# Two layers with a chunked two-way scan: the state part of a chunk placed beside the inverse of the next chunk

## The reference

```python
def rwkv_scan(state0, f, d, reverse):
    ...
    def step(S, inp):
        r_t, w_t, k_t, v_t, kk_t, b_t = inp
        sa = -jnp.einsum("bhvk,bhk->bhv", S, kk_t)
        S = S * w_t[:, :, None, :] + sa[..., None] * b_t[:, :, None, :] + v_t[..., None] * k_t[:, :, None, :]
        return S, jnp.einsum("bhvk,bhk->bhv", S, r_t)
```

## Time and profile before

| what | value |
|---|---|
| median of three runs | 2203.51 us |
| the runs | 2200.98 to 2205.61 us |
| span of the profiled execution (first to last instruction) | 2192.6 us |
| share of the span in which PE was busy | 89% |
| share of VectorE, ScalarE, GpSimd | 47%, 34%, 14% |
| mean granted TensorE clock | 0.954 |
| scan of layer 0, first to last matmul | 213.1 to 436.9 us |
| scan of layer 1, first to last matmul | 1462.7 to 1678.5 us |

### The profile page before, as it was taken

How to read it: one execution, slowest core, us unless ns; L and a number is a source line. 1 busy time by engine, 2 the same in 40 slices (tenths; PEclk the granted TensorE clock), 3 DMA queues, 4 the chain that set the end, 5 groups by cost and what they waited for, 6 DMA issues and landing times. The chain is left out here.

```text
span 2192.6 us, 51555 instructions
## 1 busy us (share of the span) xinstructions
PE 1952.2 (89%) x22829; PEld 1569.6 (72%) x22829; DVE 1039.9 (47%) x1721; ACT 754.5 (34%) x1380; POOL 298.3 (14%) x381
## 2 busy tenths in 40 slices
PE   4985888898899999899998998968888899998988
PEld 1662878753578887688886766737876458998988
DVE  1536666572733333433332216476665363545544
ACT  1334333224632322332221114353332453435432
POOL 2103333202000111100001001043331120100000
PEclk7997999999999999999999998979999999999999
DMA  8513000020113333133236742000001114554543
GB/s 326 188 49 115 5 4 4 4 72 1 39 61 97 90 102 106 39 115 110 83 115 238 286 163 60 28 1 4 5 5 44 32 39 145 177 172 144 176 152 125
DMA packets 143452, 203.96 MB, mean 93 GB/s; under 512 B 6718, under 2 KB 123672, under 8 KB 137088
## 3 DMA queue, kind: packets, MB, share of 16 engines
q1 hardware_dynamic: 141728, 198.96, 27.1%
q0 software_dynamic: 1504, 1.71, 0.2%
HBM read 199.61 MB, written 1.05 MB: 92 GB/s over the span
## 5 line engine op out<-in xcount | busy, mean ns | idle before, releaser
L330 DVE TENSOR_TENSOR W_low<-RING,W_high 128x1024 fp32r<-128x1024 f32 x268 | 329.2, 1232 | 464.2 <-ACT W_high L327 463.9
L366 PE MATMUL BANK<-H_high,W_high 128*128 128x512 f32 (+2 forms) x1472 | 520.2, 353 | 19.2 <-ACT H_high L632 8.9
L368 PE MATMUL BANK<-H_high,W_low 128*128 128x512 f32 (+2 forms) x1472 | 515.5, 350 | 0.0
L367 PE MATMUL BANK<-H_low,W_high 128*128 128x512 f32 (+2 forms) x1472 | 515.4, 350 | 0.0
L327 ACT ACTIVATE W_high<-RING 128x1024 fp32r<-128x1024 f32 x268 | 281.1, 1052 | 598.2 <-PE BANK L368 576.8
L366 PEld LDWEIGHTS BANK<-H_high,W_high 128*128 128x128 f32 (+1 forms) x1472 | 280.5, 191 | 67.4 <-issue 26.4
L367 PEld LDWEIGHTS BANK<-H_low,W_high 128*128 128x128 f32 (+1 forms) x1472 | 280.8, 191 | 36.8 <-issue 0.9
L368 PEld LDWEIGHTS BANK<-H_high,W_low 128*128 128x128 f32 (+1 forms) x1472 | 280.2, 190 | 37.3
L1259 PE MATMUL BANK<-RING,WORK 64*64 64x64 f32 x4352 | 162.6, 222 | 13.8 <-issue 7.9
L1259 PEld LDWEIGHTS BANK<-RING,WORK 64*64 64x64 f32 x4352 | 144.7, 134 | 26.7 <-issue 9.8
L1259 PE MATMUL BANK<-RING 64*64 64x64 f32 (+1 forms) x3840 | 101.5, 255 | 43.9 <-DVE RING L1165 30.2
(11 more groups left out here) (307 smaller groups left out, 2824.9 us busy)
## 6 DMA issues: line engine op xcount, KB each, us to landing
RING<-w_in_dram SPq DMA_DIRECT2D x46, 1024.0 KB, 5.4
RING<-w_ffn_in_dram SPq DMA_DIRECT2D x44, 1024.0 KB, 5.2
lation_weights_ffn<-w_mod_dram SPq DMA_DIRECT2D x24, 1024.0 KB, 6.2
RING<-w_ffn_out_dram SPq DMA_DIRECT2D x20, 1024.0 KB, 5.1
tion_weights_opening<-w_mod_dram SPq DMA_DIRECT2D x8, 1024.0 KB, 8.5
ulation_weights_norm<-w_mod_dram SPq DMA_DIRECT2D x8, 1024.0 KB, 7.0
on_weights_features<-w_mod_dram SPq DMA_DIRECT2D x8, 1024.0 KB, 5.0
RING<-w_out_dram SPq DMA_DIRECT2D x8, 1024.0 KB, 5.2
```

The lines of the kernel that those rows point to most:

```text
L330: low_ready.mark(nc.vector.tensor_tensor(self.part(1, c), self.raw(c), self.part(0, c).bitcast(FP32), ALU.subtract))
L366: nc.tensor.matmul(out, w[0], x[0], start=start, stop=False)
L367: nc.tensor.matmul(out, w[0], x[1], start=False, stop=False)
L368: return nc.tensor.matmul(out, w[1], x[0], start=False, stop=stop)
```

## The change

The scan is reordered in such a way that step i of the loop does the inverse of chunk i and, beside it, the state part of chunk b = i - 1. The first step has no state part, and after the last step the state part of chunk 7 follows by itself (without state products, which nothing reads). On TensorE the groups of the state part stand behind the merge products of the levels: level 1 the first half of the keys' turn; level 2 its second half and the first half of W; level 3 the second half of W and both SA; level 4 the two halves of Y; at level 5 the turn of the values together with the last term of Y stands between X1 and the merge products, and the state products behind them.

Since two chunks are now under way, several tiles exist twice (`GRAM_X`, `BK_TOK`, `ARB`, half of the inverse, four columns of `DEC`), the PSUM banks are given out anew (the keys' second gram and all turned tiles share one bank, the state part has one of its own), and the decayed queries and keys are written over `EXCL`, `INCL` and `BB` rather than to tiles of their own, so that the copy `keep` (L1171, VectorE) is gone. The two subtractions of `exponents` go from VectorE to GpSimd. The unit is added to half of the first level on GpSimd (new signal `s_eye`) and to the other half on VectorE. For the first two chunks of each segment Y is put by a ScalarE copy rather than added by VectorE, and the clearing of Y on GpSimd (L1080) is gone. `DEC`, the chunk's decay, is computed one chunk ahead with the other exponentials.

```diff
-    DEC = [sb(f"decay_{d}", [P, PAIRS]) for d in range(NDIR)]
+    DEC = [sb(f"decay_{d}", [P, 4, PAIRS]) for d in range(NDIR)]
...
+    K_DECAYED = [scratch(PAIRS, HD) for _ in range(NDIR)]
+    T_PARTS = [scratch(3, PAIRS, HD) for _ in range(NDIR)]
+    GRAM_X = [[scratch(PAIRS, 2, HD) for _ in range(2)] for _ in range(NDIR)]
...
             @block.gpsimd
...
                             s_lm[d].mark(nc.gpsimd.tensor_tensor(LM[d], LTS[d], lanes(level_mask(d, l)), ALU.mult))
-                        if more and l in (3, 5):
-                            d = (l - 3) // 2
-                            operands(i + 1, t[d], d)
+                            if l == 1:
+                                pool.wait_ge(*at_step(s_first[d], i, 1, 1))
+                                s_eye[d].mark(nc.gpsimd.tensor_tensor(inverse(d, i)[:, 1], inverse(d, i)[:, 1], lanes(eye_heads[:]), ALU.add))
+                        if i + 1 < STEPS:
+                            if l == 1:
+                                exponents(i + 1)
+                            if l >= 4:
+                                operands(i + 1, l - 4)
...
             @block.scalar
...
+                        if more and l == 1:
+                            exps(i + 1, 1)
+                        for d in range(NDIR):
+                            if l == 2:
+                                bk_token_major(i, d)
+                            if b >= 0 and l == 3:
+                                w_out(b, d)
+                            if b >= 0 and l == 4:
+                                sa_out(b, d)
+                            if l == NL and has_y(b) and puts(b):
+                                y_put(b, d)
+                    for d in range(NDIR):
+                        v_token_major(i, d)
...
             @block.vector
...
+                        for d in range(NDIR):
+                            merge_level(i, l, d)
+                        if l == 1 and b >= 1:
+                            new_states(b - 1)
+                        if more and l in (2, 3):
+                            operands(i + 1, l - 2)
+                new_states(STEPS - 2)
+                for d in range(NDIR):
+                    y_add(STEPS - 1, d)
...
             @block.tensor
...
+                    grams(i)
+                    level(i, 1, None, in_turn(turned[0]))
+                    level(i, 2, None, in_turn(turned[1], w[0]))
+                    level(i, 3, None, in_turn(w[1], sa[0], sa[1]))
+                    level(i, 4, None, in_turn(y[0], y[1]))
+                    level(i, NL, y_and_v, ds[0])
+                    if ds[1]:
+                        ds[1]()
+                b = STEPS - 1
+                for part in w_products(b):
+                    part()
+                for d in range(NDIR):
+                    sa_product(b, d)
+                for part in y_products(b):
+                    part()
+                for d in range(NDIR):
+                    s_y[d].mark(side_by_side(HD, y_from_sa(b, d))[0])
```

More of the change, by code:

```diff
@@ L243, in carve @@
             return flat
-        names = "abcd"[:len(shape)]
+        names = "abcde"[:len(shape)]
         return flat.rearrange(f"p ({' '.join(names)}) -> p {' '.join(names)}",
@@ L1019, in chunk_of, with tokens_of @@
         return CHUNK * i if d == 0 else (CHUNK * (N - 1) + (TOK - CHUNK) * i) % TOK
+    def tokens_of(d, i):
+        return slice(chunk_of(d, i), chunk_of(d, i) + CHUNK)
     def scan(context_y):
         y0 = 0 if context_y else N
[L1028 to L1034, removed]
+        has_y = lambda b: y0 <= b < STEPS
+        puts = lambda b: b % N < N // 2
+        puts_before = lambda b: sum(puts(x) for x in range(y0, b))
+        adds_before = lambda b: sum(not puts(x) for x in range(y0, b))
         def level_mask(d, l):
@@ L1098, in exps @@
[L1098 to L1107 removed]
+                    nc.scalar.activation(DEC[d][:, i % 4].unsqueeze(2), INCL[d][:, :, at.stop - 1:at.stop], ACT.Exp, scale=-KAPPA)
@@ L1109, in step, with y_put @@
+                def y_put(b, d):
+                    act.wait_ge(*at_step(s_y[d], b - y0, 1, 1))
+                    s_y_put[d].mark(nc.scalar.activation(Y[:, :, tokens_of(d, b)], pairs(B_STATE(d), HALF), ACT.Copy))
+                for d in range(NDIR):
+                    exps(0, d)
+                for i in range(STEPS):
+                    b, more = i - 1, i + 1 < STEPS
+                    if more:
+                        exps(i + 1, 0)
                     for d in range(NDIR):
@@ L1231, in _ @@
                 nc.vector.memset(STATE[0], 0.0)
                 s_init.mark(nc.vector.memset(STATE[1], 0.0))
-                exponents(0, chunk_of(1, 0))
                 for d in range(NDIR):
-                    operands(0, chunk_of(d, 0), d)
-                run(dve, step)
+                    operands(0, d)
+                for i in range(STEPS):
+                    b, more = i - 1, i + 1 < STEPS
+                    gram_out(i, 0)
+                    for d in range(NDIR):
+                        first_level(i, d)
+                        arb_out(i, d)
+                    gram_out(i, 1)
+                    for l in range(1, LEVELS):
+                        if l == NL and has_y(b) and not puts(b):
+                            for d in range(NDIR):
+                                y_add(b, d)
+                        for d in range(NDIR):
+                            merge_level(i, l, d)
[3 more added lines that the diff above has]
+                            operands(i + 1, l - 2)
@@ L1238, in _ @@
+                new_states(STEPS - 2)
+                for d in range(NDIR):
+                    y_add(STEPS - 1, d)
             @block.tensor
             def _(pe):
-                def each(bank, at, width, lhs, rhs, stride=None):
-                    stride = stride or width
-                    for j in range(PAIRS):
-                        for rows in (UP, DOWN):
-                            last = nc.tensor.matmul(BANK[rows, bank, at + j * stride:at + j * stride + width],
-                                                    lhs(j)[rows], rhs(j)[rows], start=True, stop=True)
-                    return last
```

444 lines of the change are left out of this document (225 added, 219 removed).

## The result

The changed kernel takes 2211.43 us (median of 20 runs, 2203.55 to 2222.97), the kernel before, on the same chips, 2200.52 (20 runs). The ratio is 1.0058, 95% interval 1.0044 to 1.0073: slower by 12.8 us (the two medians differ by 10.9).

What follows compares the result with a forecast made beforehand. The arrival of TensorE's instruction blocks was taken to bound the scans. Ends -1.4 and pace -6.5 gave -8 us: 2203.5 - 8 = 2195.5 us, the forecast's own range 2185 to 2207, the whole range 2172 to 2212.

Steps and rivals of the forecast that it cites:

- What bounds the scans: Both scans: their length is set by the arrival of blocks of some 255 TensorE instructions, about 3.85 us apiece; chance 0.67.
- the first rival: Both scans: instruction arrival is hidden and the chain decides, steps of 22.3 us, the kernel at 2126; chance 0.10.
- C: The experiments' rival for the scans: a plain chain of waits, instructions in time; 16 matmuls more cost 0 to +3 us.
- Instructions: Both scans: state products of the last chunk left out, net 0.9 blocks, -3.5 us, then replaced by the ends' -1.4.
- Chain of a step: Each scan step: the chain takes about 22.3 us against 28, its first half 11.3 against 12.6 of arrival, so instructions are late next.
- the signs of being right: Profile after: 57 or 58 packets in scan 0, "issue" idle time grown, TensorE's waits for ScalarE and VectorE shrunk.
- Ends: End of each scan: the last chunk's state part alone, 8.3 us against 7.7 + 1.3; -0.7 each, -1.4 in both.
- Pace of the blocks: Both scans: blocks come 3.8 us apart against 3.83 and 3.89; -6.5 us, between -17.6 and +4.6; the granted clock makes no term.
- The slower rival: First half of a step: GpSimd's queue becomes the bound, 1 us longer in 15 steps, 2211; chance 0.15.
- the upper end: Pace in both scans: every block comes late, 3.87 to 3.94 us apart as late ones did before; +4.6 us.

Runs made afterwards that it cites:

- after_extra16: The changed kernel with the second half of the keys' turn issued twice in each step, 16 more matmuls: ratio 1.0111 to the kernel before.
- before_extra16: The kernel before with 16 turns of the keys issued twice in each step, 16 more matmuls: ratio 1.0069 to the kernel before.
- after_less16: The changed kernel without 16 of the 48 turns of a step: ratio 0.9998 to the kernel before.
- after_noend: The changed kernel without the last chunk's state part in both scans: ratio 0.9940 to the kernel before, 26 ± 7 us less than the changed kernel.
- after_warm: The changed kernel with 48 more products that nobody reads at the end of each scan, order kept: ratio 1.0024 to the kernel before.
- after_epi: The changed kernel with Y's products in the last chunk's state part put right behind W, into another bank: ratio 1.0013 to the kernel before.
- after_first: The changed kernel with VectorE's masks and units before its other evictions, and both GpSimd masks before both units: ratio 1.0076 to the kernel before.

## Why the prediction was wrong

*What bounds the scans* was right: the arrival of blocks. `after_extra16`, `before_extra16` and `after_less16` speak for it, and the first rival, instructions hidden, is gone with C. These three runs alone leave another reading: 16 products also keep TensorE busy for some 0.6 us (half of the 1.23 in the earlier trace rows), 9.5 us in 16 steps, so a scan bound by TensorE's own work would have answered much alike. The trace of the kernel before decides between them. From the end of one gap of the earlier trace rows to the next:
```profile
310.87:314.70 3.83, 3.30 (x126) 3.00 (x127) 2.77 (x7) 1.78 (x6) 2.36 (x3) 1.00 0.02 4
314.70:318.60 3.90, 2.51 (x126) 2.17 (x125) 2.23 (x7) 0.61 (x3) 0.00 (x0) 1.00 0.02 4
318.60:322.55 3.95, 3.45 (x126) 3.07 (x126) 0.51 (x2) 1.43 (x4) 0.00 (x0) 1.00 0.02 4
```
Whatever the program does there, 251 to 253 records of TensorE lie between two gaps; in all 16 pairs of neighbouring "issue" gaps of scan 0 that are less than 5 us apart it is 250 to 254. And all 29 "issue" gaps of that scan end 2.5 us (spread 0.2) after the start of a packet on the instruction queue. Neither TensorE's own work nor a wait for another engine would end after a fixed number of records and a fixed time behind a packet.

*Instructions*: right, 180 packets for 181.

*Chain of a step*: its use failed. It was added up over half a step, 11.3 us against 12.6 of arrival, and taken as covered. TensorE's waits for other engines did not go into that cover: they rose from 5.8 to 9.9 us in seven steps, nearly all in two places, ahead of X1 of level 1 and ahead of SA, where the signs of being right had them shrink. What is late next was not the instructions alone. A likely reason is that a wait isn't set against 12.6 us but stands within one block of 3.9; no run shows it.

*Ends*: the first of two steps that failed, by size. The two ends were put at 2 x 8.3 = 16.6 us; `after_noend` says 26, with some 7 us of uncertainty, and the profile 12.2 + 11.9 = 24.1. The list of parts was the right chain, but W, SA, Y and the last term were priced at 3.7 us from rows of mid-scan and took 8.8. At full clock, in scan 1 of `after_warm`, they took 5.3: so 1.6 us is a price too low at any clock, and some 3.5 is the granted clock, of which the pace term says that it "makes no term". The clock had fallen just before the lone chain began and did not come back while it ran. Where it came back in time and Y stood ahead of SA, in `after_epi`, the end took 8.6.

*Pace of the blocks*: the other step that failed, and in sign. Of the 21 us between the forecast's -8 and the measured +12.8 it makes some 11, the ends 9. -6.5 us was forecast, between -17.6 and +4.6. Of the 12.8 us measured, the ends make -1.4 + 9.4 = +8, which leaves about +5, with the ends' uncertainty of 7. `after_epi` gives it more closely: its ends of 8.6 and 8.5 are near the forecast's 8.3, so the end term is -0.9 there, and the +2.9 us (-0.7 to +6.4) that it still loses to the kernel before leave +3.8 (0.2 to 7.3) for the pace. The steps on one chip agree, 6 x (0.3 to 1.3), +2 to +8. So the upper end held, the one of the late blocks in the earlier trace rows, and nothing here shows that closing up TensorE's work brings a block sooner. By the "issue" gaps a late block takes the same time in both kernels: 1.3 us from the end of a gap to the next packet's start, 2.5 from there to the end of the next gap, 3.8 together, and that was nearly the mean before. 3.8 had been chosen near the means without a row below them. What made the mean longer, 3.96 and 4.00 us, is open.

*The slower rival* named the right side and nearly the right time by the wrong mechanism, which is luck (its sum has a slip: 15 less 8 is +7, not +8). That the measured time lies in the forecast's range is luck too: the range reached up to 2212 for that rival's sake.

Open is which waits lengthen the steps of scan 0: one attempt to shorten them moved them, the other, which filled them, gave -5.7 us with overlapping intervals and no shorter scan in its profile.

## What to carry to other kernels

Where many small matmuls run, count instructions per block before chains: filling TensorE's idle time bought nothing clear of noise here, and each block saved or added was worth some 3 to 4 us. Idle time for which the profile names no cause, that ends after the same number of records each time and the same time behind a packet of the instruction queue, is a wait for instructions. Reordering one chunk's work beside the next chunk's leaves a lone chain at the end of each loop; price it at the clock that TensorE is granted there, not at that of the middle, and put its independent products into one run. A wait that disappears and comes back as "issue" speaks for the supply as the limit.

## What had not been expected of the hardware

In scan 0 of the changed kernel the packets on the instruction queue start 1.3 us (mean of 37) after the end of an "issue" gap, and such gaps end 2.5 us after a packet's start; in the kernel before it is 1.3 and 2.5 as well. In the scans no packet started sooner than 3.2 us after the one before, in any run here. It looks as if TensorE asks for the next block only when it is well into the one at hand.

Alternating transposes and products stood 0.17 to 0.21 us apart at each change of kind, where products follow each other after 0.06, as above.

VectorE's unit of 256 columns takes 0.43 us in direction 0 and 0.58 in direction 1 of the changed kernel (297.05, 298.44), and 0.94 in `after_first` (299.22). GpSimd's masks and units ran beside it in all three: in the slower two they had begun first (298.02, 299.15), in the first VectorE had, and there GpSimd's unit took 0.97 us (297.09), where its masks take 0.73.
